# Both output projections begun four chunks ahead of their phase, on two of their four token tiles

## The chip, the cores and the metric

The kernel runs on one core of a Trainium2 chip. The metric is device time in microseconds (us), the median of several executions. Everything is float32.

## What is computed

One inference step of a two-layer decoder: 512 prompt tokens and 64 sample tokens (8 sequences of 8 new tokens), model width 1024. Each layer is a token mixer, its output projection, and a mixture of experts, with an RMS norm ahead of both parts and a residual add behind both.

```
layer 0 mixer: softmax attention with a forget bias, 16 heads of 64; the 8 sample
               sequences also attend to 512 cached keys each (paged)
layer 1 mixer: mLSTM, 8 heads, key 64, value 128; the 8 sample sequences update
               a stored state C (8 x 8 x 64 x 128), which is an output;
               h = h * rsqrt(mean(h*h) + eps) * head_norm * sigmoid(o), per head
x = x + mixer_out @ w_out                      # 1024 x 1024: the output projection
x = x + sum over a token's 2 of 32 experts of (silu(h @ gate) * (h @ up)) @ down
                                               # gate, up 1024 x 256, down 256 x 1024 each
```

The experts' weights are 3 MB for one expert and 96 MB for one layer, and all of them are read.

## The kernel before, in words

The program is a row of seven phases: `fox_project`, `fox_attention`, `out_and_experts(0)`, `mlstm_project`, `mlstm_cells`, `out_and_experts(1)`, `finish`. In each phase every engine has a list of its own, and semaphores order the lists. Between phases all five engines meet (`run`): each drains, adds to the semaphore `together`, and waits until all five have done so. Nothing of a phase begins before the last engine has ended the one ahead. The order in a phase is written out by hand; there is no planner.

PSUM is one tile `ps` of 8 banks of 512 columns. Tokens are in five tiles (`NT`): four of 128 prompt tokens and one of the 64 sample tokens. `turned[:, c, tokens]` holds the mixer's result with chunk `c` (of 8, `KC`) of the 1024 channels on the partitions. It is the stationary operand of the output projection, `w[:, c, :]` is the moving one.

**The output projection**, `multiply_out` in `out_and_experts`: for each chunk `c`, once it has landed, and each prompt tile `n`, two products of 128 x 512 go to banks `2n` and `2n + 1`. All eight banks are full at the end. Each program product of this width is two MATMUL records in the trace, so 64 products are 128 records of L1233. The sample tokens follow (L1240). The vector engine then adds the banks to `x` (`add_tile`, L1472), and norm, transposes, router logits, routing, and a gather of rows follow in a chain, until the first `gate_up`. The experts run in 16 steps of two experts. Weights of steps 0 and 1 are asked for at the phase's start, of step 2 once the projection has ended (`multiplied`), and of every later step when a slot comes free: the first at `gu_half`, in the middle of the first `gate_up`.

In layer 0 the weights `w0` of the projection lie in a part of the attention's memory that has come free. The sync engine (SP) asks for their chunks in `fox_attention` (`w_chunk`, L659): 0 and 1 after the keys of the seventh sequence have been turned (`kt_done`), 2 to 5 after the values' product of the seventh (`do_done`), 6 and 7 after the maximum of the eighth (`dtopped`). In layer 1 the weights are placed in the slot `gu[2]` of the third expert pair, and SP asks for all eight chunks at the start of `out_and_experts(1)` (L1128); the tensor engine runs four products on constants meanwhile (`idle_products`, L186; eight records).

**The end of `fox_attention`** handles the sample sequences `b` one after the other. The tensor engine's list in step `b`: turn half of the keys (L766), turn the weights of `b - 1` (`d_turn_weights`, L777 and L778), turn the other half, multiply the values of `b - 1` (`d_values`, L790, 40 records), scores of `b` (`d_scores`, L808), turn the result of `b - 1` (`d_turn_out`, L816). The scalar engine takes the exponentials and copies the turned weights (L894, L901), the vector engine takes the maximum (L967), scales the result (L985) and places it in `turned` (`d_place`, L993). `d_turn_weights` of `b` waits for the exponentials and for the placing of `b - 1`. In the last step (`b` = 8) no keys and no scores are left. Keys use banks 0 to 3.

**The end of `mlstm_cells`**: heads are handled in four pairs. For each half of a pair the tensor engine multiplies the values (L2246) and adds the update of one sample state (`add_outer`, L2258); the vector engine divides (`heads`), the scalar engine squares (L2365), GpSimd roots and scales the gate (`root_pair`, L2154 to L2159), the vector engine multiplies (`stage`, L2459), the tensor engine turns the pair into banks 2 and 3 (`flip`, L2273), and the scalar engine copies it to two chunks of `turned` (`keep_flipped`, L2371). `flip` of the last pair is the last item of the tensor engine's list. SP writes out each sample state when it has been added to (L2129), and waits for all writes (`c_out`) at the end.

Of the kernel before, what the change touches and what calls it, by code (L numbers as in the profile page):

```python
# [20 lines left out]
P = 128  # L21
# [95 lines left out]
def trunk(nc, i, o):  # L117

    with ExitStack() as ctx:
# [57 lines left out]
        back_in = [[lasting(f"back_in{layer}_{n}") for n in range(NT)] for layer in range(2)]  # L177
        w0_in, x_again = [lasting(f"w0_in{c}") for c in range(KC)], lasting("x_again")
# [29 lines left out]
        def fox():  # L208
            dx = ExitStack()
            pages = sb("pages", [1, SB * NPAGE], I32, where=dx)  # L210
            arena = sb("fox_arena", [P, FOX_W], where=dx)

            def part(name, w=None):
                at, full = FOX_AT[name]
                return arena[:, at:at + (w or full)]

            qT = part("qT").rearrange("p (c t) -> p c t", c=PAIRS)
            kT = part("kT").rearrange("p (c t) -> p c t", c=PAIRS)
            v = part("v").rearrange("p (n d) -> p n d", n=NT)
# [5 lines left out]
            out_and_experts(0, i["fox_w_out"][0], w0)  # L225

# [345 lines left out]
        def fox_attention(part, qT, kT, v, pages, w0):  # L572
# [48 lines left out]
            def sp_(sp):  # L621
# [36 lines left out]
                def w_chunk(c):  # L658
                    sp.dma_start(w0[:, c, :], i["fox_w_out"][0][c * P:(c + 1) * P, :]).then_inc(w0_in[c], 16)  # L659

# [133 lines left out]
            def d_scores(pe, b):  # L794
# [15 lines left out]
                mm.then_inc(ds_done, 1)  # L810

            def d_turn_out(pe, b):

# [5 lines left out]
            def pe_(pe):  # L819
# [12 lines left out]
                for b in range(SB + 1):  # L832
# [186 lines left out]

        def out_and_experts(layer, w_dram, w_early=None):  # L1020

# [4 lines left out]
            SLOTS = 3  # L1026
            gu = [sb(tag + f"gu{s}", [P, 2, 2, KC, HID], where=mx) for s in range(SLOTS)]
            wd = [sb(tag + f"wd{s}", [P, 2, 2, D], where=mx) for s in range(SLOTS - 1)]
            wd.append(rows[:, 0:4, :].rearrange("p (h m) d -> p h m d", h=2))
            w = w_early if w_early is not None else gu[2][:].rearrange("p h k c n -> p (h k c n)").rearrange("p (c d) -> p c d", d=D)  # L1030
            xT = rows[:, L, :].rearrange("p (c t) -> p c t", t=P)
# [32 lines left out]

            w_in = [sem(tag + f"w_in{c}") for c in range(KC)] if layer else w0_in
            multiplied, added = sem(tag + "multiplied"), sem(tag + "added")
# [589 lines left out]

        def mlstm_project(qT, kT, knat, vaug, og, nat, carryb, C, qs, ws, tri01, negg_dram, small):

            L = NT - 1
            HT = TOK // 2  # L1660
            hnorm = sb("hnorm", [P, D], where=small)
            wblk = sb("mwblk", [P, 3, KC, 512], where=small)
            wg = ws
# [34 lines left out]
            def load_block(sp, k):  # L1698
                b = BLOCKS[k]
                sp.dma_start(wblk[:, k % 3], w_view[:, :, b * 512:b * 512 + 512]).then_inc(w_in[k % 3], 16)  # L1700

# [64 lines left out]
            def narrow(pe, g, k, bank, done):  # L1766

                for c in range(KC):
                    for half in range(2):
                        mm = pe.matmul(ps[:, bank + half, 0:HT], wblk[:, k % 3, c, g * P:(g + 1) * P],  # L1770
                                       turned[:, c, half * HT:(half + 1) * HT], start=(c == 0), stop=(c == KC - 1))
# [37 lines left out]
            def wide(pe, first, done, kept):  # L1809

                for m in range(2 * L):
# [6 lines left out]
                    for c in range(KC):  # L1818
                        mm = pe.matmul(ps[:, m % 4, :], turned[:, c, n * P:(n + 1) * P], wblk[:, k % 3, c, :],  # L1819
                                       start=(c == 0), stop=(c == KC - 1))  # L1820
# [7 lines left out]
                for c in range(KC):  # L1828
                    for blk in range(2):
                        mm = pe.matmul(ps[blk * SAMP:(blk + 1) * SAMP, 4 + blk, :], turned[:, c, PROMPT:TOK],  # L1830
                                       wblk[:, (first + blk) % 3, c, :], start=(c == 0), stop=(c == KC - 1))
                mm.then_inc(done, 1)
# [9 lines left out]
            def first_half(pe, half, chunks):  # L1842

                for c in chunks:
                    mm = pe.matmul(ps[:, 4 + half, 0:HT], wblk[:, 0, c, 0:P], turned[:, c, half * HT:(half + 1) * HT],
                                   start=(c == 0), stop=(c == KC - 1))
# [198 lines left out]
        def mlstm():  # L2045
            mx = ExitStack()
            qT = sb("mqT", [P, MPAIRS, TOK], where=mx)
            kT = sb("mkT", [P, MPAIRS, TOK], where=mx)
            knat = sb("mknat", [P, NT, MH * MK], where=mx)
# [9 lines left out]
            small = ExitStack()  # L2059
            mlstm_project(qT, kT, knat, vaug, og, nat, carryb, C, qs, ws, tri01, negg_dram, small)  # L2060
            small.close()
            mlstm_cells(qT, kT, knat, vaug, og, nat, carryb, C, qs, ws, tri01, negg_dram)
            mx.close()
            out_and_experts(1, i["mlstm_w_out"][0])

# [12 lines left out]

        def mlstm_cells(qT, kT, knat, vaug, og, nat, carryb, C, qs, ws, tri01, negg_dram):

# [6 lines left out]
            tri = [tri01[:, 0], tri01[:, 1], tri23[:, 0], tri23[:, 1]]  # L2087
            qm = sb("qm", [P, MPAIRS, SB, SAMP], where=ms_)
            cp = sb("cp", [P, MPAIRS, A], where=ms_)
            hb = sb("mhb", [P, 2, KT * 2 * MV], where=ms_)  # L2090
            staged = sb("mstaged", [P, 2, KT * 2 * MV], where=ms_)
            kwm = sb("kwm", [SAMP, 2, MH * MK], where=ms_)
            dn = sb("mdn", [P, 3, MPAIRS, 2, KT], where=ms_)
            ss = sb("mss", [P, 3, MPAIRS, KT, 2], where=ms_)
            sdn = sb("msdn", [SAMP, 3, 2, 2, 2], where=ms_)
            sss = sb("msss", [SAMP, 3, MH], where=ms_)
            NN = (SB + 1) * MPAIRS
            nn = sb("mnn", [P, NN], where=ms_)
            n_rows = sb("mn_rows", [NN, P], where=ms_)

# [9 lines left out]
                sem("s_h"), sem("s_sq"), sem("s_meaned"), sem("s_rooted"), sem("s_og"), sem("s_st"), sem("s_flipped"), sem("s_f_kept"))  # L2110
            kwm_ready, c_scaled, dc_done, dc_added, c_out = sem("s_kwm"), sem("s_scaled"), sem("s_dc"), sem("s_dc_added"), sem("s_c_out")
            PER_PAIR = 6

# [4 lines left out]
            def sp_(sp):  # L2118
# [3 lines left out]
                sp.wait_ge(cp_kept, 1)  # L2122
                sp.dma_start(o["C_prompt"].rearrange("a b (p h) d v -> (h d) (a b p) v", h=2), cp[:, :, 0:MV]).then_inc(c_out, 16)
# [6 lines left out]
                sp.wait_ge(c_out, 16 * (SB + 3))  # L2130

# [178 lines left out]
            def pe_(pe):  # L2310
# [20 lines left out]
                for p in range(1, MPAIRS + 1):  # L2331
# [11 lines left out]
                    else:  # L2343
                        flip(pe, p - 2)
                flip(pe, MPAIRS - 1)


# [146 lines left out]
        def finish():  # L2494

            fin = ExitStack()
            L = NT - 1
            sb("f_held", [P, 2 * NT + 1, D], where=fin)
            gl = last_gain[1]
# [114 lines left out]
```

## Time and profile before

| | us |
|---|---|
| time, median of 3 runs | 1422.75 (1417.06 to 1423.74) |
| the profiled execution, its own time | 1428.57 |
| its span in the profile | 1426.7 |
| tensor engine busy | 1237.4 (87%) |
| vector engine busy | 370.4 (26%) |
| scalar engine busy | 246.7 (17%) |
| GpSimd busy | 214.4 (15%) |
| read from and written to memory | 248 GB/s over the span |

The page of the profile divides the span into 40 slices. Its line for the DMA engines reads 8 to 9 tenths over long stretches in both expert phases and 0 to 3 tenths in others, so the means of the table say little of any one stage. The chain of waits (section 4 of the page) is followed back from the last instruction, and its pieces can be listed in order of time.

### The profile page before, as it was taken

Reading aid. Unit: us, or ns where it says so; the run is one execution under the profiler, and the core shown is the slowest. Engines: PE = TensorE matmul, PEld = TensorE weight load, DVE = VectorE, ACT = ScalarE, POOL = GpSimd, SP = SyncE. Lnnn points to the kernel's source line nnn. Section 1 sums busy time; section 2 is a strip of 40 time slices with the busy share of each in tenths; the row PEclk is TensorE's granted clock in tenths of the full one; section 3 lists DMA queues with packets and bytes.
Section 4 is the critical chain, followed back from the end, with each engine's and each line's share of the span. In section 5 each row is a group of like instructions: output and inputs, shape, how many; then the busy total and the mean of one; then the engine's idle time right before and its main releaser. Section 6 shows DMA issues by size and latency. Waiting matters only on the chain.

```text
span 1426.7 us, 16246 instructions
## 1 busy us (share of the span) xinstructions
PE 1237.4 (87%) x6285; PEld 654.8 (46%) x6285; DVE 370.4 (26%) x793; ACT 246.7 (17%) x572; POOL 214.4 (15%) x268
## 2 busy tenths in 40 slices
PE   8999999879699899778868999998879989977790
PEld 5764575557444533233324764444744543333330
DVE  4231003545311621111114400112710541111115
ACT  2000004653200201000003201014410300100001
POOL 2300002322100111111001000212920011111102
PEclk9999999999999999988988999999989999998995
DMA  8320504859975689999957130303148579999965
GB/s 282 102 62 7 179 13 137 266 183 362 344 282 224 250 302 420 419 419 420 410 221 270 60 105 18 121 12 82 39 146 352 190 253 417 419 420 419 419 277 207
DMA packets 103676, 339.96 MB, mean 238 GB/s; under 512 B 21454, under 2 KB 40082, under 8 KB 79786
## 3 DMA queue, kind: packets, MB, share of 16 engines
q1 hardware_dynamic: 88456, 302.84, 55.8%
q0 software_dynamic: 14848, 35.94, 7.0%
q8 instruction: 53, 0.87, 0.3%
q14 instruction: 29, 0.24, 0.1%
q10 hardware_dynamic: 290, 0.07, 0.0%
HBM read 322.18 MB, written 31.31 MB: 248 GB/s over the span
## 4 chain that ended last, share of the span: by engine, by line
PE 54%; SPq 16%; DMA 12%; DVE 7%; issue 4%; POOL 3%; ACT 2%; POOLq 2%; DVEq 0%; ACTq 0%
SPq L1096 10%; PE ps L1819 8%; PE ps L1233 8%; PE ps L1308 7%; PE ps L458 4%; DMA moe_gu<-in_moe_w_up 4%; SPq L1118 4%; PE ps L436 4%; PE ps L1770 4%; DMA fox_arena<-negs_rows 3%; PE ps L1326 3%; PE ps L351 2%; DMA moe_wd<-in_moe_w_down 1%; PE ps L748 1%; PE ps L1830 1%
## 5 line engine op out<-in xcount | busy, mean ns | idle before, releaser
L1308 PE MATMUL ps<-moe_gu,rows 128*64 128x512 f32 x1024 | 243.6, 630 | 57.1 <-DMA moe_gu<-in_moe_w_up 53.8
L1308 PEld LDWEIGHTS ps<-moe_gu,rows 128*64 128x64 f32 x1024 | 80.5, 145 | 199.8 <-issue 191.1
L1819 PE MATMUL ps<-mwblk,turned 128*128 128x512 f32 x256 | 111.5, 593 | 2.2 <-DVE vaug L2022 1.5
L1595 DVE TENSOR_TENSOR turned<-turned,ps 128x256 f32<-128x256 f32 x32 | 13.5, 421 | 304.7 <-ACT turned L1411 304.7
L1192 POOL DMA_INDIRECT expert_rows<-turned,moe_row x32 | 32.1, 1004 | 392.3 <-ACT turned L1421 358.8
L1326 PE MATMUL ps<-moe_wd,moe_rowsel 128*64 128x512 f32 x352 | 80.4, 598 | 2.3 <-DMA moe_wd<-in_moe_w_down 1.3
L1819 PEld LDWEIGHTS ps<-mwblk,turned 128*128 128x128 f32 x256 | 48.0, 190 | 61.1 <-issue 57.4
L1411 ACT ACTIVATE turned<-ps 128x256 f32<-128x256 f32 x32 | 12.3, 384 | 302.4 <-PE ps L1308 302.4
L458 PE MATMUL ps<-turned,fox_arena 128*128 128x288 f32 x256 | 62.3, 406 | 0.0
L436 PE MATMUL ps<-fox_arena,turned 128*128 128x512 f32 x128 | 59.0, 619 | 2.9 <-issue 2.9
L1233 PE MATMUL ps<-fox_arena,turned 128*128 128x512 f32 x128 | 55.2, 593 | 0.7 <-DVEq L2564 0.7
L351 PE MATMUL ps<-turned,fox_arena 128*128 128x288 f32 x224 | 55.2, 406 | 0.0
L1233 PE MATMUL ps<-moe_gu,turned 128*128 128x512 f32 x128 | 55.2, 593 | 0.0
L458 PEld LDWEIGHTS ps<-turned,fox_arena 128*128 128x128 f32 x256 | 48.6, 190 | 14.1 <-issue 0.8
L1770 PE MATMUL ps<-turned,mwblk 128*128 128x288 f32 x224 | 54.5, 406 | 0.0
L237 POOL TENSOR_TENSOR fox_arena<-fox_arena,cst 128x256 f32<-128x256 f32 x32 | 23.0, 728 | 201.2 <-DMA fox_arena<-negc_rows 201.0
L186 PE MATMUL ps<-cst 128*128 128x512 f32 x68 | 40.0, 731 | 9.5 <-POOLq L2564 8.3
L1770 PEld LDWEIGHTS ps<-turned,mwblk 128*128 128x128 f32 x224 | 42.6, 190 | 11.8
L351 PEld LDWEIGHTS ps<-turned,fox_arena 128*128 128x128 f32 x224 | 42.2, 190 | 11.4
L1600 DVE COPY turned<-ps 128x512 f32<-128x512 f32 x32 | 22.1, 691 | 88.0 <-PE ps L1326 88.0
L1185 POOL DMA_INDIRECT turned<-h_rows,moe_row x32 | 33.2, 1038 | 76.6 <-DVE moe_row L1554 44.1
L928 DVE CUSTOM_DVE_ANT_0 fox_arena<-ps,fox_arena 128x128 f32<-128x128 f32 (+3 forms) x64 | 28.2, 479 | 62.9 <-PE ps L725 62.9
(357 smaller groups left out, 1567.5 us busy)
## 6 DMA issues: line engine op xcount, KB each, us to landing
moe_gu<-in_moe_w_gate SPq DMA_DIRECT2D x56, 1024.0 KB, 22.3
moe_gu<-in_moe_w_up SPq DMA_DIRECT2D x56, 1024.0 KB, 23.9
moe_wd<-in_moe_w_down SPq DMA_DIRECT2D x44, 1024.0 KB, 25.0
rows<-in_moe_w_down SPq DMA_DIRECT2D x20, 1024.0 KB, 22.9
fox_arena<-in_cache_v POOLq DMA_DIRECT2D x32, 512.0 KB, 13.1
fox_arena<-in_fox_w_in SPq DMA_DIRECT2D x6, 2048.0 KB, 10.3
mwblk<-in_mlstm_w_in SPq DMA_DIRECT2D x6, 2048.0 KB, 8.6
fox_arena<-in_cache_k SPq DMA_DIRECT2D x20, 512.0 KB, 9.7
```

The costliest lines, as they stand in the source:

```text
L186: pe.matmul(ps[:, bank, :], ident, const("ones")[:, 0:512], start=True, stop=True)
L351: mm = pe.matmul(ps[:, 2 * (g % 3) + half, 0:HT], wblk[:, g // 4, c, (g % 4) * P:(g % 4 + 1) * P], turned[:, c, half * HT:(half + 1) * HT] ...
L436: mm = pe.matmul(ps[:, m % 4, :], turned[:, c, n * P:(n + 1) * P], wblk[:, (2 + blk) % 3, c, :], start=(c == 0), stop=(c == KC - 1))
L458: mm = pe.matmul(ps[:, 2 * ((g + 2) % 4) + half, 0:HT], wblk[:, (4 + g // 4) % 3, c, (g % 4) * P:(g % 4 + 1) * P], turned[:, c, half * HT: ...
L1096: sp.dma_start(gu[p % SLOTS][:, half, k], i[name][layer, 2 * p + half].rearrange("(p c) n -> p c n", c=KC)).then_inc(gu_in[p % SLOTS], 16)
L1118: sp.dma_start(wd[p % SLOTS][:, half], i["moe_w_down"][layer, 2 * p + half].rearrange("(p c) n -> p c n", c=2)).then_inc(down_in[p % SLOTS ...
L1185: pool.indirect_dma_start(xg[:, s, :], None, h_dram[layer], bass.IndirectOffsetOnAxis(ap=rows_of(0, p), axis=0), bounds_check=TOK - 1, oob ...
L1233: mm = pe.matmul(ps[:, 2 * n + half, :], turned[:, c, n * P:(n + 1) * P], w[:, c, half * 512:half * 512 + 512], start=(c == 0), stop=(c == ...
L1308: mm = pe.matmul(ps[h, 2 + p % 2, :].rearrange("s (k f) -> s k f", k=2), xT[:, c, h], gu[s][:, half, :, c, :], start=(c == 0), stop=(c == ...
L1326: mm = pe.matmul(ps[h, 5 + n, :], aT[p % 2][:, m, h], wd[s][:, half, m, n * 512:(n + 1) * 512], start=(m == 0), stop=(m == 1))
L1770: mm = pe.matmul(ps[:, bank + half, 0:HT], wblk[:, k % 3, c, g * P:(g + 1) * P], turned[:, c, half * HT:(half + 1) * HT], start=(c == 0), ...
L1819: mm = pe.matmul(ps[:, m % 4, :], turned[:, c, n * P:(n + 1) * P], wblk[:, k % 3, c, :], start=(c == 0), stop=(c == KC - 1))
```

## The change

In `fox_attention`, tiles 0 and 1 of the projection are begun: chunk 0 behind the scores of the eighth sequence, chunk 1 behind its turned weights, chunk 2 behind its values' product, chunk 3 behind the last turn. In `mlstm_cells`, chunks 0 to 3 of tile 0 are put ahead of the last `flip`, and those of tile 2 behind it. The products go to the banks in which the projection goes on, which skips them. In layer 1 the weights get a place in an arena over the queries, keys and a zone: the zone holds the third weight block of `mlstm_project` and then the small tiles of `mlstm_cells`. SP asks for chunks 0 to 5 behind the last scores, 6 and 7 near the end, ahead of the last state's write. The four idle products are taken out. The slot `gu[2]` of layer 1 is laid over the same addresses.

```diff
+        BEGUN = ((0, 1), (0, 2))
+        def project_tile(pe, layer, w, n, chunks):
+            for c in chunks:
+                pe.wait_ge(out_in[c], 16 * (layer + 1))
+                for half in range(2):
+                    pe.matmul(ps[:, 2 * n + half, :], turned[:, c, n * P:(n + 1) * P], w[:, c, half * 512:half * 512 + 512],
+                              start=(c == 0), stop=False)
...
             # fox_attention
+            def begin(pe, c):
+                for n in BEGUN[0]:
+                    project_tile(pe, 0, w0, n, [c])
...
                     if b:
                         d_turn_weights(pe, b - 1)
+                    if b == SB:
+                        begin(pe, 1)
                     if b < SB:
                         d_turn_keys(pe, b, range(4, PAIRS))
                     if b:
                         d_values(pe, b - 1)
                     if b < SB:
                         d_scores(pe, b)
+                    if b == SB - 1:
+                        begin(pe, 0)
+                    elif b == SB:
+                        begin(pe, 2)
                     if b:
                         d_turn_out(pe, b - 1)
+                begin(pe, 3)
...
             # out_and_experts, SP's list
-                for c in range(KC if layer else 0):
-                    sp.dma_start(w[:, c, :], w_dram[c * P:(c + 1) * P, :]).then_inc(w_in[c], 16)
...
             def multiply_out(pe):
-                if layer:
-                    idle_products(pe, 4, 0)
                 for c in range(KC):
-                    pe.wait_ge(w_in[c], 16)
+                    pe.wait_ge(out_in[c], 16 * (layer + 1))
                     for n in range(L):
+                        if n in BEGUN[layer] and c < KC // 2:
+                            continue
...
             # mlstm_cells, SP's list
+                def w_chunk(c):
+                    sp.dma_start(w1[:, c, :], i["mlstm_w_out"][0][c * P:(c + 1) * P, :]).then_inc(out_in[c], 16)
                 for b in range(SB):
+                    if b == 4:
+                        sp.wait_ge(nd_done, 2)
+                        sp.wait_ge(s_done, 3 * MPAIRS)
+                        for c in range(6):
+                            w_chunk(c)
+                    if b == SB - 1:
+                        sp.wait_ge(dc_done, SB - 1)
+                        w_chunk(6)
+                        sp.wait_ge(cp_out, 16)
+                        sp.wait_ge(dc_done, SB)
+                        w_chunk(7)
                     sp.wait_ge(dc_added, b + 1)
                     sp.dma_start(o["C_sample"][0, b].rearrange("(p h) d v -> (h d) p v", h=2), C[:, b, :, 0:MV]).then_inc(c_out, 16)
...
             # mlstm_cells, the tensor engine's list
+                pe.wait_ge(f_kept, 2)
+                project_tile(pe, 1, w1, BEGUN[1][0], range(KC // 2))
                 flip(pe, MPAIRS - 1)
+                pe.wait_ge(h_ready, 2 * MPAIRS)
+                project_tile(pe, 1, w1, BEGUN[1][1], range(KC // 2))
...
         # mlstm
+            QW, ZONE = MPAIRS * TOK, KC * 512
+            arena = sb("m_arena", [P, 2 * QW + ZONE], where=mx)
+            zone = arena[:, 2 * QW:2 * QW + ZONE]
+            w1 = arena[:, 0:KC * D].rearrange("p (c d) -> p c d", d=D)
```

## Rows read from the trace of the kernel before

**Rows 1.** Page, costliest groups: busy us, mean ns of one, idle before.

```profile
L1233 PE MATMUL ps<-fox_arena,turned 128*128 128x512 f32 x128 | 55.2, 593 | 0.7 <-DVEq L2564 0.7
```

**Rows 2.** Chain of waits in order of time: start us, us, what.

```profile
408.42 55.17 PE ps L1233 x128
...
661.46 28.76 DMA moe_gu<-in_moe_w_up
...
1054.71 5.22 DMA moe_gu<-in_mlstm_w_out
1059.98 55.20 PE ps L1233 x128
```

**Rows 3.** Windows: us, busy PE, PEld, DVE, ACT, POOL; PE clock, DMA share, GB/s.

```profile
450.00:460.00 10.00, 10.00 (x25) 4.38 (x24) 1.22 (x1) 0.20 (x1) 0.00 (x0) 1.00 0.00 0
...
600.00:700.00 100.00, 78.88 (x342) 30.85 (x342) 14.03 (x18) 7.54 (x18) 12.14 (x12) 0.90 1.02 420
...
1160.00:1200.00 40.00, 39.03 (x192) 14.97 (x188) 7.96 (x10) 3.67 (x9) 5.04 (x5) 1.00 1.01 392
```

**Rows 4.** Timeline, end of `fox_attention`: start us, us, engine, line, what, idle before.

```profile
399.18 0.40 PE L808 MATMUL ps<-fox_arena 128*32 128x64 f32 x16
...
399.51 0.44 PE L816 MATMUL ps<-cst,fox_arena 128*128 128x128 f32 x2
...
400.33 0.47 DVE L993 COPY turned<-ps 64x64 f32<-64x64 f32 x2
...
401.37 0.66 PE L777 MATMUL ps<-cst,fox_arena 128*128 128x128 f32 x4 [1.43 <-ACT fox_arena L894]
...
402.83 3.83 PE L790 MATMUL ps<-fox_arena 128*32 128x256 f32 x40 [0.69 <-ACT fox_arena L901]
...
407.27 0.44 PE L816 MATMUL ps<-cst,fox_arena 128*128 128x128 f32 x2 [0.62 <-DVE fox_arena L985]
407.75 0.48 DVE L993 COPY turned<-ps 64x64 f32<-64x64 f32 x2 [0.53 <-PE ps L816]
```

**Rows 5.** Timeline: the same product for an earlier sequence.

```profile
326.25 2.37 PE L790 MATMUL ps<-fox_arena 128*32 128x256 f32 x40
```

**Rows 6.** Windows of the end of `fox_attention`, columns as in rows 3.

```profile
399.50:401.40 1.90, 0.47 (x11) 0.23 (x3) 1.17 (x5) 0.87 (x2) 0.00 (x0) 1.00 0.85 280
...
402.80:404.00 1.20, 1.17 (x12) 0.59 (x16) 0.00 (x0) 0.00 (x0) 0.00 (x0) 0.50 1.02 365
```

**Rows 7.** Line L659: issue ns, first and last start us; then landing.

```profile
L659 SPq DMA_DIRECT2D fox_arena<-in_fox_w_out x8: 341/430/1005, 379.5 to 400.8; - x8
...
DMA to landing us min/median/max: 4.1/7.7/14.2
```

**Rows 8.** Timeline, end of `mlstm_cells`, columns as in rows 4.

```profile
1028.86 0.92 PE L2212 MATMUL ps<-mqT,mkT 64*128 64x256 f32 x8
...
1044.18 1.09 PE L2273 MATMUL ps<-cst,mstaged 128*128 128x128 f32 x8
...
1051.55 1.97 PE L2273 MATMUL ps<-cst,mstaged 128*128 128x128 f32 x8 [6.28 <-DVE mstaged L2459]
1053.55 1.02 ACT L2371 ACTIVATE turned<-ps 128x1024 f32<-128x1024 f32 x1 [6.46 <-PE ps L2273]
...
1054.75 5.18 PE L186 MATMUL ps<-cst 128*128 128x512 f32 x8 [1.24 <-ACTq L2564]
```

**Rows 9.** Windows of the end of `mlstm_cells`, columns as in rows 3.

```profile
1043.30:1045.30 2.00, 1.97 (x24) 1.56 (x22) 1.68 (x8) 0.43 (x4) 0.00 (x0) 1.00 0.42 131
...
1048.00:1051.50 3.50, 0.00 (x0) 0.00 (x0) 1.22 (x1) 0.00 (x0) 2.16 (x2) 0.50 0.00 0
```

**Rows 10.** Line L1128, its landing.

```profile
DMA to landing us min/median/max: 5.2/7.9/9.5
```

**Rows 11.** Line L2129: duration ns, first and last start us.

```profile
L2129 SPq DMA_DIRECT2D out_C_sample<-Cs x8: 372/372/388, 1006.4 to 1045.7; - x8
```

**Rows 12.** Line L631, its landing.

```profile
DMA to landing us min/median/max: 5.7/15.3/27.0
```

More of the change, by code:

```diff
@@ L177, in trunk @@
         back_in = [[lasting(f"back_in{layer}_{n}") for n in range(NT)] for layer in range(2)]
-        w0_in, x_again = [lasting(f"w0_in{c}") for c in range(KC)], lasting("x_again")
+        out_in, x_again = [lasting(f"out_in{c}") for c in range(KC)], lasting("x_again")
         W0_AT = 2 * 8 * D - SB * NPAGE
@@ L1017, in fox_attention, with out_and_experts @@
             pa.close()
-        def out_and_experts(layer, w_dram, w_early=None):
+        def out_and_experts(layer, w):
             tag = f"moe{layer}_"
@@ L1026, in out_and_experts @@
             SLOTS = 3
-            gu = [sb(tag + f"gu{s}", [P, 2, 2, KC, HID], where=mx) for s in range(SLOTS)]
+            gu = {s: sb(tag + f"gu{s}", [P, 2, 2, KC, HID], where=mx) for s in ((2, 0, 1) if layer else (0, 1, 2))}
             wd = [sb(tag + f"wd{s}", [P, 2, 2, D], where=mx) for s in range(SLOTS - 1)]
             wd.append(rows[:, 0:4, :].rearrange("p (h m) d -> p h m d", h=2))
-            w = w_early if w_early is not None else gu[2][:].rearrange("p h k c n -> p (h k c n)").rearrange("p (c d) -> p c d", d=D)
             xT = rows[:, L, :].rearrange("p (c t) -> p c t", t=P)
@@ L1063, in out_and_experts @@
             ctl = sb(tag + "ctl", [1, MORE + 1], I32, where=mx)
-            w_in = [sem(tag + f"w_in{c}") for c in range(KC)] if layer else w0_in
             multiplied, added = sem(tag + "multiplied"), sem(tag + "added")
@@ L1655, in combine, with mlstm_project @@
                                      ).then_inc(combined, 1)
-        def mlstm_project(qT, kT, knat, vaug, og, nat, carryb, C, qs, ws, tri01, negg_dram, small):
+        def mlstm_project(qT, kT, knat, vaug, og, nat, carryb, C, qs, ws, tri01, negg_dram, small, zone):
             L = NT - 1
@@ L1661, in mlstm_project @@
             hnorm = sb("hnorm", [P, D], where=small)
-            wblk = sb("mwblk", [P, 3, KC, 512], where=small)
+            wfirst = sb("mwblk", [P, 2, KC, 512], where=small)
+            wblk = [wfirst[:, 0], wfirst[:, 1], zone.rearrange("p (c n) -> p c n", c=KC)]
             wg = ws
@@ L1769, in narrow @@
                     for half in range(2):
-                        mm = pe.matmul(ps[:, bank + half, 0:HT], wblk[:, k % 3, c, g * P:(g + 1) * P],
+                        mm = pe.matmul(ps[:, bank + half, 0:HT], wblk[k % 3][:, c, g * P:(g + 1) * P],
                                        turned[:, c, half * HT:(half + 1) * HT], start=(c == 0), stop=(c == KC - 1))
@@ L1818, in wide @@
                     for c in range(KC):
-                        mm = pe.matmul(ps[:, m % 4, :], turned[:, c, n * P:(n + 1) * P], wblk[:, k % 3, c, :],
+                        mm = pe.matmul(ps[:, m % 4, :], turned[:, c, n * P:(n + 1) * P], wblk[k % 3][:, c, :],
                                        start=(c == 0), stop=(c == KC - 1))
@@ L1830, in wide @@
                         mm = pe.matmul(ps[blk * SAMP:(blk + 1) * SAMP, 4 + blk, :], turned[:, c, PROMPT:TOK],
-                                       wblk[:, (first + blk) % 3, c, :], start=(c == 0), stop=(c == KC - 1))
+                                       wblk[(first + blk) % 3][:, c, :], start=(c == 0), stop=(c == KC - 1))
                 mm.then_inc(done, 1)
@@ L1844, in first_half @@
                 for c in chunks:
-                    mm = pe.matmul(ps[:, 4 + half, 0:HT], wblk[:, 0, c, 0:P], turned[:, c, half * HT:(half + 1) * HT],
+                    mm = pe.matmul(ps[:, 4 + half, 0:HT], wblk[0][:, c, 0:P], turned[:, c, half * HT:(half + 1) * HT],
                                    start=(c == 0), stop=(c == KC - 1))
@@ L2046, in mlstm @@
             mx = ExitStack()
-            qT = sb("mqT", [P, MPAIRS, TOK], where=mx)
-            kT = sb("mkT", [P, MPAIRS, TOK], where=mx)
+            QW, ZONE = MPAIRS * TOK, KC * 512
+            arena = sb("m_arena", [P, 2 * QW + ZONE], where=mx)
+            qT = arena[:, 0:QW].rearrange("p (c t) -> p c t", t=TOK)
+            kT = arena[:, QW:2 * QW].rearrange("p (c t) -> p c t", t=TOK)
+            zone = arena[:, 2 * QW:2 * QW + ZONE]
+            w1 = arena[:, 0:KC * D].rearrange("p (c d) -> p c d", d=D)
             knat = sb("mknat", [P, NT, MH * MK], where=mx)
@@ L2059, in mlstm @@
             small = ExitStack()
-            mlstm_project(qT, kT, knat, vaug, og, nat, carryb, C, qs, ws, tri01, negg_dram, small)
+            mlstm_project(qT, kT, knat, vaug, og, nat, carryb, C, qs, ws, tri01, negg_dram, small, zone)
             small.close()
-            mlstm_cells(qT, kT, knat, vaug, og, nat, carryb, C, qs, ws, tri01, negg_dram)
+            mlstm_cells(qT, kT, knat, vaug, og, nat, carryb, C, qs, ws, tri01, negg_dram, zone, w1)
             mx.close()
-            out_and_experts(1, i["mlstm_w_out"][0])
+            out_and_experts(1, w1)
         def gate_rows_in(sp, tri, p, k, negg_dram, landed):
@@ L2077, in mask_gate_rows, with mlstm_cells @@
             pool.tensor_tensor(own, own, const("neg_causal_t").unsqueeze(1).broadcast_to([P, 2, P]), ALU.add).then_inc(masked, 1)
-        def mlstm_cells(qT, kT, knat, vaug, og, nat, carryb, C, qs, ws, tri01, negg_dram):
+        def mlstm_cells(qT, kT, knat, vaug, og, nat, carryb, C, qs, ws, tri01, negg_dram, zone, w1):
             ms_ = ExitStack()
@@ L2087, in mlstm_cells @@
             tri = [tri01[:, 0], tri01[:, 1], tri23[:, 0], tri23[:, 1]]
-            qm = sb("qm", [P, MPAIRS, SB, SAMP], where=ms_)
-            cp = sb("cp", [P, MPAIRS, A], where=ms_)
+            NN = (SB + 1) * MPAIRS
+            places, at = {}, 0
+            for name, width in (("qm", MPAIRS * SB * SAMP), ("kwm", 2 * MH * MK), ("cp", MPAIRS * A), ("dn", 3 * MPAIRS * 2 * KT),
+                                ("ss", 3 * MPAIRS * KT * 2), ("sdn", 24), ("sss", 3 * MH), ("nn", NN), ("n_rows", P)):
+                places[name] = zone[:, at:at + width]
+                at += width
+            qm = places["qm"].rearrange("p (c b t) -> p c b t", c=MPAIRS, b=SB)
+            cp = places["cp"].rearrange("p (c a) -> p c a", a=A)
             hb = sb("mhb", [P, 2, KT * 2 * MV], where=ms_)
             staged = sb("mstaged", [P, 2, KT * 2 * MV], where=ms_)
[L2092 to L2099, printed above, removed]
+            kwm = places["kwm"][0:SAMP].rearrange("p (u n) -> p u n", u=2)
+            dn = places["dn"].rearrange("p (k c h t) -> p k c h t", k=3, c=MPAIRS, h=2)
+            ss = places["ss"].rearrange("p (k c t h) -> p k c t h", k=3, c=MPAIRS, h=2)
+            sdn = places["sdn"][0:SAMP].rearrange("p (k c r j) -> p k c r j", k=3, c=2, r=2)
+            sss = places["sss"][0:SAMP].rearrange("p (k h) -> p k h", k=3)
+            nn, n_rows = places["nn"], places["n_rows"][0:NN]
             tri_in, masked = [sem(f"mtri_in{p}") for p in (2, 3)], sem("m2_masked")
@@ L2497, in finish @@
             L = NT - 1
-            sb("f_held", [P, 2 * NT + 1, D], where=fin)
+            sb("f_held", [P, KC + 2 * NT + 1, D], where=fin)
             gl = last_gain[1]
```

11 lines of the change are left out of this document (6 added, 5 removed).

## The prediction, made before the changed kernel was seen

> **What bounds the kernel now.** Read the chain of waits first. In the projection of either layer it is one unbroken piece of tensor work: 55.17 us from 408.42 and 55.20 us from 1059.98 [rows 2]. Ahead of the second, 5.22 us go to the DMA that brings the first weight chunk. Later the chain runs through the expert weights (28.76 us in one piece at 661.46). Then the windows [rows 3]: while the experts run, the DMA engines are busy all the time (share 1.02 at 420 GB/s from 600 to 700; 1.01 at 392 in the second layer), but from 450 to 460, in the projection, they move nothing (0.00). The weights of steps 0 and 1 have landed by then, and the next wait for the projection's end or for a slot that the first `gate_up` frees. So the stream's length is fixed by bytes, but its start hangs on the tensor engine through projection, norm, routing and gather. A microsecond taken out ahead of that chain moves the stream and the end by a microsecond. The sum is therefore made on one quantity per layer: when the last product of L1233 ends, now 463.59 and 1115.18 (start plus duration, rows 2).
>
> **What is moved.** A product of the program is two records: 128 records take 55.17 us, 0.431 us each, with the idle before them only 0.7 us [rows 1, 2]. (The mean of 593 ns of one record is its latency, not its spacing.) Two tiles x four chunks x two halves are 16 products, 32 records, 13.8 us in each layer; 96 records, 41.4 us, stay. The work is the same in sum; it pays only where it fills time in which the tensor engine stood still, or ran at the low clock.
>
> **Layer 0, step by step.** The eighth scores end at 399.58 (399.18 + 0.40) and the turn L816 can start at once [rows 4]. New: `begin(0)`, 8 records, 3.45 us, so the turn ends not at 399.95 but near 403.4. The placing (two copies of L993, 0.47 us) follows, and the turned weights wait for it: 403.95 in place of 401.37. Here the new work costs 2.6 us on the path; it covers the 1.4 us that L777 waited for the exponentials. L777 and L778 take 0.77 us (they end at 402.14, as L790's wait of 0.69 us shows): 404.7. `begin(1)`: 408.2; it hides both copies of L901 and L978. Values: before they began at 402.83 and took 3.88 us until 406.71, and the granted clock was 0.50 there [rows 6], which is the lower of the two levels, 1.2 GHz, after an engine that had stood still 1.43 and 0.69 us. The same 40 records took 2.37 us for an earlier sequence [rows 5]. With the gaps filled the engine works from 399.6 on with one gap of about 0.55 us, so I take 2.37: they end at 410.6. `begin(2)` to 414.0 hides the scaling L985 (0.62 us of wait). The turn, 0.45: 414.5. `begin(3)` to 417.9 hides the last placing. Then the meeting of the engines: from the end of the placing, 408.22, to the first product, 408.42, it took 0.2 us [rows 2, 4]; behind a product 0.15 more for its latency over its spacing: first product of the next phase at 418.25. 41.4 us more: 459.65. **Before 463.59: 3.9 us earlier.** Bounds: if the values stay at the low clock (3.88), 2.4; if neither the gap of 0.55 nor the 0.35 at the meeting is seen, 4.8.
>
> The chunks are in time. SP's waits (`kt_done`, `do_done`, `dtopped`) all end ahead of `begin(0)`, so nothing of SP's list moves. Chunks 0 and 1, asked for at 379.5, are there 14.2 us later at the latest, at 394 [rows 7], and the first is needed at 399.6. The last is asked for at 400.8 and lands by the median of 7.7 us at 408.5, at worst at 415.0; chunk 2 is needed at 410.6, chunk 3 at 414.5, chunk 7 far later. Phase 3 begins 9.8 us later than before, and with it the loads of steps 0 and 1; they have ended before 450 now [rows 3], so near 460 then, still ahead of step 2's, which ask at the projection's end.
>
> **Layer 1.** The last turn but one ends at 1045.27; the tensor engine then stands still 6.28 us until the last pair has been rooted and staged [rows 8]. New: tile 0, 16 records, 6.9 us, to 1052.2. Both waits ahead are over: the second pair was copied long before, and chunks 0 to 3 are asked for when the last scores end, at 1029.78, behind the state write of b = 3. The same eight loads, asked for together, landed 5.2 to 9.5 us after their issue [rows 10]; issue of six takes some 4 us, so even the sixth is there by 1043.5. The last `flip` begins 0.65 us late, at 1052.2, but the clock: it is 1.00 while the turn before it runs, and 0.50 after 1048, when the engine has stood still [rows 9]. In the new order the engine doesn't stand still. The turn that took 1.97 us takes 1.09 as the one at 1044.18 [rows 8]: 1053.3. Tile 2, 6.9 us: 1060.2, beside the copy of the last pair (L2371, 1.02 us) and the meeting. First product of the next phase 0.35 us later: 1060.55, 0.6 us later than before (1059.98), since the wait for the chunk (5.22) and the idle products (5.18) are gone from the path. Then 41.4 us: 1101.95. **Before 1115.18: 13.2 us earlier.** Bounds: 12.3 if the last turn stays at 1.97; 13.8 if the meeting costs nothing more than before.
>
> The other edits: taking out the idle products costs nothing once the engine is busy without a break into the meeting (if it fell cold there, the four cost some 1.7 us: 5.18 less the 8 x 0.431 of full speed). Third weight block, `qm`, `kwm` and the rest lie at other addresses, same sizes, same instructions: nothing. The expert loads of layer 1 no longer stand behind 4 MB of w: nothing, they are early anyway. SP waits for the last scores ahead of the write of state 4, which waits for a later addition anyway.
>
> **Sum.** 3.9 + 13.2 = 17.1 us. Profiled execution: 1428.57 (span 1426.7 and 1.9 around it) - 17.1 = 1411.5. The runs' median is 1422.75, 5.8 below the profiled one, so 1422.75 - 17.1 = **1405.6 us**. Likeliest case alone: 14.7 to 18.6 us less (the two sums of bounds), 1404 to 1408, and some 4 us each way for the spread of the runs (1417.06 to 1423.74).
>
> **Rivals.**
>
> *A: the write of the last state holds the phase.* SP ends `mlstm_cells` only when all state writes have landed. The write of b = 7 now goes out behind two chunks of 512 KB asked for at about 1043 and 1044.3; before it was alone, issued at 1045.7 [rows 11]. For: the same queue has brought a broadcast transfer of 256 KB after 27.0 us [rows 12]. Against: that was under a full DMA load, here the engines are nearly idle, and the chunks took at most 9.5 us [rows 10]: 1053.8, then the write, well before 1060.2. The Trainium skill, "DMA: Bandwidth & Descriptors", section "Queues, rings and completion order", says that a semaphore increment lands only after all earlier writes of that DMA engine; by it the state's write can't be reported before chunk 7 has landed. No row shows such a pair. By it and rows 10 the report comes after 1053.8, and the sum stays. Price: two chunks at 27 us each, one behind the other, from 1044: 1098, a start 38.6 us late in place of 0.6, less 13.8 and 3.9: 20.9 us slower than before, 1443.6. It decides from 1077.6 on (1059.98 + 13.8 + 3.9).
>
> *B: the begun products run at the low clock.* The idle products show the price: the first records at 1054.75 ran at half speed, eight in 5.18 us. At 0.864 each (5.18 less four at 0.431, over four), the 64 moved records cost 27.7 us more, less the 17.1 gained: 10.6 us slower, 1433.4. It decides from 40 slow records on. Against: in both places the work follows work at clock 1.00 [rows 6, 9] without a break.
>
> *C: only layer 1 pays.* The tail of `fox_attention` has small gaps, and four blocks of 3.45 us each stand on its path; if the waits behind them grow by what they cover (a chunk late by 4 us, a gap that opens elsewhere), 3.9 goes: 1409.5.
>
> *D: the stream doesn't follow.* If the expert weights end by bytes alone whatever starts them, nothing changes: 1422.75. The zero DMA share from 450 to 460 speaks against it.
>
> **How the numbers follow.** Forecast 0.80, C 0.08, D 0.05, A 0.04, B 0.03. What a measurement can tell from no change is about 0.5%, 7.1 us. Faster: forecast and C, 0.88. Same: D and the mild form of A and B, 0.08. Slower: 0.04. The range takes in the likeliest case with its spread and C with its own: 1398 to 1413.
>
> **What would show it.** In the trace after: 32 records of the new helper's line in `fox_attention`, values of the eighth sequence in some 2.4 us at clock 1.00, L1233 x96 from about 418 to 460; in `mlstm_cells` 16 records in the gap behind 1045 and 16 behind the last turn, that turn in 1.1 us, L1233 x96 from about 1056.7 (3.9 less than 1060.55) to 1098; no idle product there; expert stream and every phase behind shifted by 3.9 and 17.1 us. Wrong: a wait of the tensor engine for a chunk, SP as the last at the meeting, or a DMA share below 1 between 600 and 700.

## The result, and the profile after

The changed kernel takes 1402.84 us (median of 4 runs, 1401.24 to 1403.18), the kernel before 1420.48 (4 runs): 17.6 us less, ratio 0.9875, 95% interval 0.9851 to 0.9898, which is 14.5 to 21.2 us. The forecast was 17.1 us less. In a later group of runs on one chip the same kernel stood at 0.9894 (0.9870 to 0.9919), which is 15.1 us less. So the runs alone confirm the forecast to some 3 us; what is said to a tenth below is read from traces.

The span of the profiled execution fell by more, from 1426.7 to 1401.2 us. Here the two traces must be put side by side from a common event, and not by their clocks' zero. Line numbers have moved: the projection is now L1251 (L1233 before), the scores L818 (L808), the values L800 (L790), the turn of the result L831 (L816); in `mlstm_cells` the values are L2289 (L2246) and the turn `flip` L2316 (L2273). The products of `project_tile` stand in the trace as L190. The chain of waits of the changed kernel (start us, us, what) answers to [rows 2]:

```profile
410.19 41.44 PE ps L1251 x96
...
1048.51 41.44 PE ps L1251 x96
```

The projection ends at 451.63 and 1089.95, where it ended at 463.59 and 1115.18: 12.0 and 25.2 us earlier. But 7.9 us of both lie ahead of the first change. The timeline of the end of `fox_attention` after it, columns as in [rows 4]:

```profile
391.28 0.41 PE L818 MATMUL ps<-fox_arena 128*32 128x64 f32 x16
391.61 3.70 PE L190 MATMUL ps<-fox_arena,turned 128*128 128x512 f32 x8
...
395.15 0.38 PE L831 MATMUL ps<-cst,fox_arena 128*128 128x128 f32 x2
...
396.77 3.60 PE L190 MATMUL ps<-fox_arena,turned 128*128 128x512 f32 x8
...
400.30 2.37 PE L800 MATMUL ps<-fox_arena 128*32 128x256 f32 x40
402.59 3.70 PE L190 MATMUL ps<-fox_arena,turned 128*128 128x512 f32 x8
...
406.35 3.60 PE L190 MATMUL ps<-fox_arena,turned 128*128 128x512 f32 x8
...
410.19 2.38 PE L1251 MATMUL ps<-fox_arena,turned 128*128 128x512 f32 x5 [0.24 <-PEq L2611]
```

The eighth scores end at 391.69 (391.28 + 0.41); before, at 399.58. No begun product precedes that point. From it to the projection's first product the kernel before needs 8.84 us, the changed one 18.50, but its projection is shorter by the 13.7 us of the moved products (41.44 in place of 55.17): 4.1 us gained in layer 0. The four blocks of L190 stand where they were put, the values take 2.37 us in place of 3.83, and the engines' meeting now waits for the tensor engine (PEq) and lasts 0.24 us.

The same for the end of `mlstm_cells`, which answers to [rows 8]:

```profile
1025.84 1.61 PE L2289 MATMUL ps<-vaug,mtri 128*128 128x129 f32 x12
1030.45 1.16 PE L2289 MATMUL ps<-vaug,mtri 128*128 128x129 f32 x8 [3.01 <-DVEq L2474]
...
1032.57 1.09 PE L2316 MATMUL ps<-cst,mstaged 128*128 128x128 f32 x8
...
1033.50 7.03 PE L190 MATMUL ps<-m_arena,turned 128*128 128x512 f32 x16
...
1040.37 1.04 PE L2316 MATMUL ps<-cst,mstaged 128*128 128x128 f32 x8
1041.24 7.03 PE L190 MATMUL ps<-m_arena,turned 128*128 128x512 f32 x16
1041.44 1.02 ACT L2418 ACTIVATE turned<-ps 128x1024 f32<-128x1024 f32 x1 [5.97 <-PE ps L2316]
```

The standing time of 6.28 us is gone, the last turn takes 1.04 us in place of 1.97, and the four idle products and the wait for the first chunk are gone too. From the start of the turn before it (1044.18; now 1032.57) to the end of the projection: 71.00 us before, 57.38 now, 13.6 us gained in layer 1. Together these are 17.7 us. That the medians give 17.6 is closer than their interval warrants, and so in part luck. Windows after, columns as in [rows 3, 9]:

```profile
403.00:409.90 6.90, 6.90 (x18) 2.83 (x16) 0.66 (x3) 0.00 (x0) 0.00 (x0) 1.00 0.26 104
...
1033.40:1040.40 7.00, 7.00 (x20) 3.12 (x19) 1.91 (x2) 2.07 (x9) 3.73 (x3) 1.00 0.58 181
1040.40:1041.40 1.00, 1.00 (x10) 1.00 (x9) 0.00 (x0) 0.00 (x0) 0.00 (x0) 1.00 0.00 0
1041.40:1048.30 6.90, 6.87 (x17) 2.69 (x15) 0.00 (x0) 1.02 (x1) 0.00 (x0) 1.00 0.00 0
...
590.00:690.00 100.00, 79.55 (x342) 30.75 (x344) 13.33 (x17) 6.67 (x16) 12.14 (x12) 0.90 1.02 419
```

The clock is 1.00 in both new stretches, and the expert stream runs as before, at share 1.02 and 419 GB/s, only earlier.

### The profile page after: what moved, and what is told of

It is laid out like the page before. It is cut to its first block, busy times and chain, and to the rows that moved or that the text cites. A ratio compares the mean times of both kernels' runs of the same rounds, so it can differ in the third digit from the quotient of the medians.

```text
span 1401.2 us, 16227 instructions
## 1 busy us (share of the span) xinstructions
PE 1232.1 (88%) x6277; PEld 653.9 (47%) x6277; DVE 370.7 (26%) x793; ACT 246.6 (18%) x572; POOL 214.5 (15%) x268
## 4 chain that ended last, share of the span: by engine, by line
PE 52%; SPq 22%; DMA 8%; DVE 7%; issue 4%; POOL 3%; ACT 2%; POOLq 2%; PEldq 1%; PEld 0%; DVEq 0%; ACTq 0%
SPq L1116 11%; PE ps L1838 8%; SPq L1138 6%; PE ps L1326 6%; PE ps L1251 6%; PE ps L468 4%; PE ps L446 4%; PE ps L1789 4%; SPq L1124 3%; DMA moe_wd<-in_moe_w_down 3%; PE ps L1344 3%; DMA fox_arena<-negs_rows 2%; PE ps L361 2%; PE ps L758 1%; PE ps L776 1%
## 5 line engine op out<-in xcount | busy, mean ns | idle before, releaser
L1326 PE MATMUL ps<-moe_gu,rows 128*64 128x512 f32 x1024 | 247.1, 638 | 54.1 <-DMA moe_gu<-in_moe_w_up 50.9
L1429 ACT ACTIVATE turned<-ps 128x256 f32<-128x256 f32 x32 | 12.3, 384 | 303.1 <-PE ps L1326 303.1
L446 PE MATMUL ps<-fox_arena,turned 128*128 128x512 f32 x128 | 56.0, 593 | 2.9 <-issue 2.9
L1838 PE MATMUL ps<-mwblk,turned 128*128 128x512 f32 x128 | 56.0, 594 | 1.5 <-DVE vaug L2041 1.5
L1838 PE MATMUL ps<-m_arena,turned 128*128 128x512 f32 x128 | 55.7, 593 | 0.7 <-ACT m_arena L1928 0.7
L468 PEld LDWEIGHTS ps<-turned,fox_arena 128*128 128x128 f32 x256 | 48.6, 190 | 14.1 <-issue 0.8
L361 PEld LDWEIGHTS ps<-turned,fox_arena 128*128 128x128 f32 x224 | 42.2, 190 | 11.4
L1344 PEld LDWEIGHTS ps<-moe_wd,moe_rowsel 128*64 128x64 f32 x352 | 23.7, 136 | 44.4 <-issue 42.0
L1316 PEld LDWEIGHTS ps<-cst,turned 128*128 128x128 f32 x256 | 31.1, 194 | 24.9 <-issue 24.3
L196 PE MATMUL ps<-cst 128*128 128x512 f32 x60 | 35.1, 725 | 8.4 <-POOLq L2611 8.4
## 6 DMA issues: line engine op xcount, KB each, us to landing
fox_arena<-in_cache_v POOLq DMA_DIRECT2D x32, 512.0 KB, 10.3
fox_arena<-in_fox_w_in SPq DMA_DIRECT2D x6, 2048.0 KB, 10.2
```

What stands on the lines that cost most here:

```text
L196: pe.matmul(ps[:, bank, :], ident, const("ones")[:, 0:512], start=True, stop=True)
L361: mm = pe.matmul(ps[:, 2 * (g % 3) + half, 0:HT], wblk[:, g // 4, c, (g % 4) * P:(g % 4 + 1) * P], turned[:, c, half * HT:(half + 1) * HT] ...
L468: mm = pe.matmul(ps[:, 2 * ((g + 2) % 4) + half, 0:HT], wblk[:, (4 + g // 4) % 3, c, (g % 4) * P:(g % 4 + 1) * P], turned[:, c, half * HT: ...
L1326: mm = pe.matmul(ps[h, 2 + p % 2, :].rearrange("s (k f) -> s k f", k=2), xT[:, c, h], gu[s][:, half, :, c, :], start=(c == 0), stop=(c == ...
L1344: mm = pe.matmul(ps[h, 5 + n, :], aT[p % 2][:, m, h], wd[s][:, half, m, n * 512:(n + 1) * 512], start=(m == 0), stop=(m == 1))
```

## The experiments

The theory: a begun product pays only the standing time it fills. Where all waits around it are filled, further products neither cost nor pay. The first rival: layer 1's gain is mostly the early weight load. The gains of the next four kernels in us are their ratios taken on the kernel before of the same group (1420.08 us); the medians give 8.9, 12.3, 4.3 and 16.1 us for them.

**Only layer 0.**

```diff
-        BEGUN = ((0, 1), (0, 2))
+        BEGUN = ((0, 1), ())
...
-                pe.wait_ge(f_kept, 2)
-                project_tile(pe, 1, w1, BEGUN[1][0], range(KC // 2))
                 flip(pe, MPAIRS - 1)
-                pe.wait_ge(h_ready, 2 * MPAIRS)
-                project_tile(pe, 1, w1, BEGUN[1][1], range(KC // 2))
```

> Only layer 0 is begun ahead; layer 1 keeps the early weight load and has no idle products, but its projection is whole in its phase. Theory (a begun product pays what it fills of standing time): layer 0 gives its 4.1 us as in the changed kernel. Layer 1: the first product starts at the phase's start, 5.2 us earlier than in the kernel before, but at the low clock, four records at 0.43 us more, so 3.5 us. Sum 7.6 us less than before, 0.9947. Rival (layer 1's gain is mostly the early load): 4.1 + some 10 = 14 us less, 0.990. In the trace: L1251 x96 in layer 0, x128 in layer 1, the first ones at clock 0.50.

1411.15 us, 0.9932 (0.9905 to 0.9958): 9.7 us less, with 7.6 inside the interval and 14 outside. The trace gives 18.49 us from the scores to the first product, as in the changed kernel. In layer 1 the projection is whole again. Timeline and chain:

```profile
1022.29 1.61 PE L2289 MATMUL ps<-vaug,mtri 128*128 128x129 f32 x12
...
1036.38 1.97 PE L2316 MATMUL ps<-cst,mstaged 128*128 128x128 f32 x8 [5.26 <-DVE mstaged L2502]
```

```profile
1039.59 56.60 PE ps L1251 x128
```

The x12 row (12 records of the values, the last work ahead of a gap of 3.01 us) stands ahead of everything that the change moves in layer 1. From its start to the end of the projection it is 73.90 us, and 77.73 before (1037.45 to 1115.18): 3.8 us gained, for 3.5 expected. The cold start cost 1.4 us here (56.60 less 55.20).

**Only layer 1.**

```diff
-        BEGUN = ((0, 1), (0, 2))
+        BEGUN = ((), (0, 2))
```

> Only layer 1 is begun ahead. Theory: 13.6 us less than before, 0.9904; the end of fox_attention as before, with the values of the eighth sequence at clock 0.50 in some 3.8 us and 8.8 us from the end of the eighth scores to the first product of the projection (18.5 in the changed kernel). Rival (the layers interact, e.g. layer 0's late phase start costs or helps the expert stream): then layer 0's share differs from 4.1 us, and this kernel is not 4.1 us slower than the changed one.

1407.78 us, 0.9913 (0.9884 to 0.9942): 12.4 us less for 13.6 expected, inside. From the scores to the first product 8.86 us (8.84 before), and the values at the low clock:

```profile
395.57 3.86 PE L800 MATMUL ps<-fox_arena 128*32 128x256 f32 x40 [0.69 <-ACT fox_arena L923]
```

In layer 1 the distance from the last turn but one to the end of the projection is 57.38 us, as in the changed kernel. In these distances the layers don't interact.

**Nothing begun**, both tuples empty, both calls in `mlstm_cells` out; the early load stays.

> Nothing is begun ahead; only the early load of layer 1's projection weights and the missing idle products stay. Theory: 3.5 us less than before, 0.9975 (5.2 us of wait for the first chunk go, 1.7 us come back because the first four records run at 1.2 GHz). Rival (the early load alone makes most of the gain): 10 us or more less, 0.993. Other rival (the idle products were worth their place: the cold start costs more than the wait saved): no change or slower.

1415.79 us, 0.9960 (0.9945 to 0.9976): 5.7 us less; 3.5 is inside the interval, 10 outside. So the rival falls: without begun products the early load is worth a few microseconds. By the trace the kernel gains 1.5 us in layer 0 (7.36 us from the scores to the first product, 8.84 before) and 2.2 us in layer 1 (75.5 us from the x12 row to the end of the projection, 77.7 before). The trace shows two things I had not expected. Timeline and windows:

```profile
391.65 0.41 PE L818 MATMUL ps<-fox_arena 128*32 128x64 f32 x16
395.30 2.37 PE L800 MATMUL ps<-fox_arena 128*32 128x256 f32 x40 [0.69 <-ACT fox_arena L923]
399.42 25.99 PE L1251 MATMUL ps<-fox_arena,turned 128*128 128x512 f32 x60 [0.70 <-DVEq L2607]
```

```profile
395.30:397.70 2.40, 2.37 (x40) 1.20 (x40) 0.00 (x0) 0.00 (x0) 0.00 (x0) 1.00 0.89 333
...
1043.90:1050.00 6.10, 6.08 (x7) 2.52 (x8) 0.15 (x2) 0.00 (x0) 0.56 (x2) 0.50 0.42 83
```

With the order of layer 0 untouched, the values ran at clock 1.00 here and took 2.37 us: the distance from scores to first product is 7.36 us, not 8.84. The low clock there is a matter of the execution. And in layer 1 the projection began cold and stayed at 0.50 for 6.1 us: its 128 records took 58.24 us in place of 55.20, 3.0 us lost for 1.7 expected.

```profile
1043.92 58.24 PE ps L1251 x128
```

So the idle products had bought between 1.4 us (the kernel with only layer 0 begun) and 3.0 us, differing from one execution to the next.

**Tile 0 only in layer 1.**

```diff
-        BEGUN = ((0, 1), (0, 2))
+        BEGUN = ((0, 1), (0,))
...
-                pe.wait_ge(h_ready, 2 * MPAIRS)
-                project_tile(pe, 1, w1, BEGUN[1][1], range(KC // 2))
```

> As the changed kernel, but in layer 1 only tile 0 is begun (ahead of the last turn), and tile 2 is not. Theory: products behind the last turn only cover the scalar engine's copy of 1.02 us and the meeting, so leaving them in the next phase costs 0.95 us: 16.7 us less than before, 0.9882. Rival (both tiles pay alike, 6.8 us each): 7 us slower than the changed kernel, 0.9925.

1404.02 us, 0.9882 (0.9852 to 0.9911): 16.8 us less for 16.7 expected; the rival's 0.9925 is outside. The runs can't resolve one microsecond, but the trace can (timeline, then chain):

```profile
1042.15 1.04 PE L2316 MATMUL ps<-cst,mstaged 128*128 128x128 f32 x8
```

```profile
1044.43 48.30 PE ps L1251 x112
```

From the start of the last turn to the end of the projection it is 50.58 us, and 49.58 in the changed kernel. So the second tile, behind the last turn, brings one microsecond by itself: its 6.9 us are only moved from one side of the meeting to the other.

**A delay in layer 0**, the test of rival D of the prediction.

```diff
             def multiply_out(pe):
 
+                if layer == 0:
+                    idle_products(pe, 12, 7)
```

> The changed kernel with 12 idle products (24 records, 10.35 us at full clock) ahead of the rest of layer 0's projection. Theory (the expert stream's start hangs on the tensor engine): everything behind comes 10.35 us later, 10.3 us slower than the changed kernel. Rival D (the stream ends by its bytes whatever starts it): no change. In the trace: the first gate and up products of layer 0 later by 10.3 us, and the end of the stream too.

1417.73 us, 0.9974 (0.9956 to 0.9991), against 0.9894 of the changed kernel in the same group: 13.2 us slower by the medians, 11.4 by the ratios. The spread is wide, so the trace decides. First expert product and the read-back of the experts' rows at the end of layer 0, changed kernel in that group, then with the delay:

```profile
496.06 7.09 PE L1326 MATMUL ps<-moe_gu,rows 128*64 128x512 f32 x32 [0.63 <-DVE rows L1607]
...
735.08 2.65 SPq L1194 DMA_DIRECT2D moe_gu<-expert_rows  x5
```

```profile
506.37 5.80 PE L1328 MATMUL ps<-moe_gu,rows 128*64 128x512 f32 x26 [0.71 <-DVE rows L1609]
...
745.51 2.68 SPq L1194 DMA_DIRECT2D moe_gu<-expert_rows  x5
```

The eighth scores end at 397.55 and 397.57, so that these times can be compared: 10.3 and 10.4 us later. The stream's end follows its start one for one, and rival D falls for layer 0. The other traces agree: in all ten the start of the first expert product lies between 490.5 and 506.4, and the read-back starts 239.0 to 239.6 us behind it. Layer 1 had no such delay run, but there the projection ends between 1085.1 and 1115.2 in the ten traces, and the span ends 310.1 to 313.2 us behind it.

**Another order in layer 0**: chunk 0 behind the turn, not ahead of it.

```diff
-                    if b == SB - 1:
-                        begin(pe, 0)
-                    elif b == SB:
+                    if b == SB:
                         begin(pe, 2)
                     if b:
                         d_turn_out(pe, b - 1)
+                    if b == SB - 1:
+                        begin(pe, 0)
```

> The changed kernel with only the order of layer 0 altered: chunk 0 behind the turn of the seventh result. Theory: the 0.66 us that the tensor engine stands ahead of the last turned weights are filled, 0.6 us less than the changed kernel; in the trace 17.9 us from the end of the eighth scores to the first product of the next phase in place of 18.5. Rival (the exponentials or the copies behind them are then late): the same 18.5.

1403.38 us, 0.9882 (0.9858 to 0.9907): not told apart from the changed kernel by the runs, but the trace gives 17.61 us (394.49 to 412.10) in place of 18.49: 0.9 us less.

**The changed kernel once more**, for comparison.

> The changed kernel once more, on the same chip as the others of this call, as their yardstick: 0.9875 of the kernel before.

1404.57 us, 0.9894 (0.9870 to 0.9919). Its trace holds a lesson of its own, at the last turn but one and in the windows around it:

```profile
1032.59 1.16 PE L2289 MATMUL ps<-vaug,mtri 128*128 128x129 f32 x8 [3.01 <-DVEq L2474]
1033.68 1.35 PE L2301 MATMUL ps<-vaug,m_arena 64*64 64x128 f32 x16
1034.96 1.97 PE L2316 MATMUL ps<-cst,mstaged 128*128 128x128 f32 x8
1036.72 7.56 PE L190 MATMUL ps<-m_arena,turned 128*128 128x512 f32 x16
```

```profile
1034.00:1036.70 2.70, 2.70 (x23) 2.37 (x19) 1.92 (x7) 1.28 (x8) 0.00 (x0) 0.57 0.85 269
```

The same 3.01 us of standing as in the first trace, but here the clock fell behind it: the turn takes 1.97 us, the tile 7.56. The x12 row ahead of that gap, before and in this trace:

```profile
1037.45 1.60 PE L2246 MATMUL ps<-vaug,mtri 128*128 128x129 f32 x12
```

```profile
1027.97 1.60 PE L2289 MATMUL ps<-vaug,mtri 128*128 128x129 f32 x12
```

From there to the end of the projection it is 65.7 us (1027.97 to 1093.70), against 64.1 in the first trace and 77.7 before.

**The same products, spread over more gaps.** With the order above, and in layer 1 two chunks of tile 0 in that gap of 3.0 us:

```diff
                 for t in range(KT):
+                    if t == 3 and p == MPAIRS - 1 and h:
+                        pe.wait_ge(f_kept, 2)
+                        project_tile(pe, 1, w1, BEGUN[1][0], range(0, 2))
                     if t == 3 and (p or h):
                         pe.wait_ge(h_ready, 2 * p + h)
...
-                pe.wait_ge(f_kept, 2)
-                project_tile(pe, 1, w1, BEGUN[1][0], range(KC // 2))
+                project_tile(pe, 1, w1, BEGUN[1][0], range(2, KC // 2))
+                pe.wait_ge(h_ready, 2 * MPAIRS)
+                project_tile(pe, 1, w1, BEGUN[1][1], range(0, 2))
                 flip(pe, MPAIRS - 1)
-                pe.wait_ge(h_ready, 2 * MPAIRS)
-                project_tile(pe, 1, w1, BEGUN[1][1], range(KC // 2))
+                project_tile(pe, 1, w1, BEGUN[1][1], range(2, KC // 2))
```

> The same begun products as the changed kernel at better places. Layer 0: chunk 0 behind the turn of the seventh sequence's result instead of ahead of it, so the placing runs beside it. Layer 1: two chunks of tile 0 into the 3.0 us that the tensor engine stands before the last product of the last pair's values; chunks 2, 3 of tile 0 and 0, 1 of tile 2 ahead of the last turn, the other two behind it. Theory: 0.6 us in layer 0 and 3.0 us in layer 1 on top of the changed kernel: 3.6 us less than it, about 0.985 of the kernel before. Rival (two chunks of 3.45 us ahead of a product that the last norm's chain needs delay that chain by more than the 0.45 us they overrun): same as the changed kernel or slower.

1398.1 us (1396.17 to 1401.64), 0.9850 (0.9829 to 0.9871): the fastest of all, 22.7 us under the kernel before and 6.5 under the changed one of the same group, by medians.

```profile
1024.22 1.61 PE L2292 MATMUL ps<-vaug,mtri 128*128 128x129 f32 x12
1025.67 3.60 PE L190 MATMUL ps<-m_arena,turned 128*128 128x512 f32 x8
...
1029.10 1.05 PE L2292 MATMUL ps<-vaug,mtri 128*128 128x129 f32 x8
...
1038.91 1.04 PE L2319 MATMUL ps<-cst,mstaged 128*128 128x128 f32 x8
1039.78 3.60 PE L190 MATMUL ps<-m_arena,turned 128*128 128x512 f32 x8
```

From the x12 row to the end of the projection (its 41.44 us begin at 1043.62) it is 60.8 us: 3.3 less than the first trace of the changed kernel (3.0 expected), 4.9 less than its second, where the clock fell. The rival is not borne out: two chunks ahead of the last values put off the last turn by 0.2 us (14.7 us from the x12 row to it, 14.5 in the first trace). With the 0.9 us of layer 0 the traces give 4.2 us less than the first trace of the changed kernel, and 5.8 less than the second; 3.6 were expected. Whether the runs differ by 4.2 or by the 6.5 of the medians is not settled, since the two intervals (up to 0.9871, from 0.9870) just touch. Of the 9.1 us between the spans of this kernel and of the second trace, 3 lie ahead of the eighth scores.

## Why the prediction was right, step by step

- **What bounds.** Right, and now shown for layer 0: a delay of 10.35 us ahead of the projection came out as 10.4 at the end of the expert stream. For layer 1 it is read from the constant distance behind the projection, and not tested by a delay.
- **Cost of the begun products.** Right: 32 records per layer, 13.8 us by the forecast, 13.7 measured; 41.44 us stay.
- **Layer 0's path.** 18.67 us from scores to first product were forecast (418.25 less 399.58), 18.50 measured (18.49 to 18.50 in all five traces with this order). No chunk was waited for.
- **The values of the eighth sequence.** The size was right, the cause only half. I charged 1.5 us of the 3.9 to filling the gaps. The kernel with nothing begun had the values at full clock too. The three traces without begun products there took 3.83, 3.86 and 2.37 us, the seven with them 2.36 or 2.37. So the high clock was seen every time with begun products and once in three times without. They don't always gain 1.5 us over the kernel before. The 4.1 us are measured against the same trace that the forecast was read from; over an execution of the kernel before in which these values run at the high clock, layer 0's gain would be 2.6.
- **Layer 1.** 13.2 forecast, 13.6 measured: the last turn was late by 0.4, not 0.65, and the meeting took 0.24, not 0.35. (The upper bound of 13.8 doesn't follow from its own condition: without the 0.35 at the meeting the sum gives 13.6.) "In the new order the engine doesn't stand still" was true only behind 1045. The gap of 3.01 us two items earlier stayed, and of six traces that keep it and have layer 1 begun, three show the low clock behind it (the last turn but one in 1.97 us in place of 1.09). In the second trace of the changed kernel layer 1's distance was 1.6 us longer, so 12.0 us of gain, and with the delay kernel 67.3 us (1039.21 to 1106.56), 10.4. My bounds (12.3 to 13.8) left that out. The loss is new: in the kernel before and the two without begun products in layer 1 the last turn starts 14.1 us behind the x12 row whether the clock fell (1.97 us for the last turn but one, twice) or not, since the engine waits there for the last pair anyway. With the gap filled by tile 0 it starts 14.5 us behind it at the high clock and 16.15 to 17.77 where the clock fell.
- **The profiled time.** 1411.5 was forecast for it, 1403.18 came. The step that failed is taking the profiled execution before as the typical one ahead of the change: it reached the end of the eighth scores at 399.58, the first trace after at 391.69 and the second at 397.55. In the kernel before and the second trace after the chain holds two waits for the broadcast rows (20.6 and 27.0 us; 19.2 and 25.9), in the early one a single wait of 23.8. Since I took the difference within the trace and put it on the median, the forecast of 1405.6 was not hurt.
- **Rivals.** A: the meeting waited for the tensor engine, not for SP; in layer 1 the chunks landed in at most 8.9 us, and in at most 10.2 in any trace. By the Trainium skill's order of completion ("DMA: Bandwidth & Descriptors", "Queues, rings and completion order") the last state's write could be held by the chunk ahead of it; no run here shows such a pair as the last at a meeting. B: cold records occurred, but few: where the clock had fallen, the 16 records of tile 0 took 7.56 to 8.25 us in place of 7.03. C: fell by the distances in the traces (18.50 us for 8.84, less 13.7 of moved work); the intervals of the runs with and without layer 0 begun overlap. D: fell.

## What to carry to other kernels

Work moved ahead over a barrier is worth the standing time it fills, not its own length: list the gaps of the engine ahead of the barrier, and cut the moved work into pieces of their size. Ask what hangs on the moved chain's end; here a stream that kept the DMA engines busy (share 1.02) passed every microsecond on, since its start was tied to that end. Compare two profiles from the last event ahead of the change, for 8 us of difference can lie before it.

## What was not expected of the hardware

The granted clock of one stretch differs between executions of the same code: behind a gap of 3.01 us it stayed at 1.00 in one trace of the changed kernel and was 0.57 in the window behind it in the next. A projection begun cold, without the idle products ahead of it, ran at 0.50 for 6.1 us and lost 3.0 us in one kernel's trace, and lost 1.4 us in another's. Small work in a gap was therefore worth 1.4 to 3 us beyond the gap, but only in some executions.
